# Hybrid decoder step: where in a unit's slot TensorE multiplies the next unit's attention scores

## The reference, cut to what matters

```python
n = rms_norm(x, g_mix)
q, k, v, xr, gr, gates = jnp.split(n @ w_in, SPLITS, axis=-1)
attn = attend(q, k, v, sb_bias)            # stick-breaking attention, 16 heads of 64, 4 kv heads
xc, rnn_buf_new = causal_dwconv(xr, rnn_buf, w_rnn_conv, b_rnn_conv)
hseq, h_last = rg_lru(xc, rnn_h0, w_rgate, b_rgate, w_igate, b_igate, rglru_lambda)
rnn = hseq * jax.nn.gelu(gr)
gate_a, gate_b = jnp.split(jax.nn.sigmoid(gates), 2, axis=-1)
x = x + (gate_a * attn + gate_b * rnn) @ w_out
# then a causal ConvFFN: up-projection, depthwise conv, gelu(ua) * ub, down-projection

def stick_breaking_weights(z, mask):       # z = q.k * scale + bias
    log_keep = jnp.where(mask, jax.nn.log_sigmoid(-z), 0.0)
    later = jnp.concatenate([log_keep[..., 1:], jnp.zeros_like(log_keep[..., :1])], axis=-1)
    tail = lax.cumsum(later, axis=z.ndim - 1, reverse=True)
    return jnp.where(mask, jnp.exp(jax.nn.log_sigmoid(z) + tail), 0.0)
```

## Time and profile before

| | |
|---|---|
| median of 3 runs | 2100.93 us |
| the profiled execution | 2100.63 us |
| its span, first to last instruction | 2098.9 us |
| TensorE busy / VectorE / ScalarE / GpSimd | 1902.7 / 1217.0 / 930.9 / 222.5 us |
| mean granted TensorE clock | 0.958 |

### The profile page before, as it was taken

How to read it: one execution, slowest core, us unless ns; L and a number is a source line. 1 busy time by engine, 2 the same in 40 slices (tenths; PEclk the granted TensorE clock), 3 DMA queues, 4 the chain that set the end, 5 groups by cost and what they waited for, 6 DMA issues and landing times. The chain is left out here.

```text
span 2098.9 us, 40932 instructions
## 1 busy us (share of the span) xinstructions
PE 1902.7 (91%) x14580; PEld 1739.5 (83%) x14580; DVE 1217.0 (58%) x1991; ACT 930.9 (44%) x1506; POOL 222.5 (11%) x106
## 2 busy tenths in 40 slices
PE   6998999899897989798995996999999999999985
PEld 5897878688786878687883776999999999999984
DVE  6101667567584858577677333655665566546645
ACT  5112676666767676667666211312222122221213
POOL 0121000000000000000003002311221122212210
PEclk9999999999998999999898997999999999999998
DMA  3334222131313232231312311211110111111104
GB/s 130 113 83 115 75 72 74 51 98 40 93 42 103 57 79 67 79 80 40 84 44 101 103 72 49 61 41 40 50 60 30 43 57 50 43 37 50 50 10 178
DMA packets 198716, 143.82 MB, mean 69 GB/s; under 512 B 58289, under 2 KB 187890, under 8 KB 198528
## 3 DMA queue, kind: packets, MB, share of 16 engines
q1 hardware_dynamic: 198554, 141.73, 23.0%
HBM read 124.31 MB, written 17.61 MB: 68 GB/s over the span
## 5 line engine op out<-in xcount | busy, mean ns | idle before, releaser
L87 PE MATMUL d_p_up<-n_hi,d_w_hi 128*128 128x346 f32 x1056 | 342.2, 324 | 15.9 <-ACT d_up L1808 8.3
L87 PE MATMUL d_p_up<-n_hi,d_w_lo 128*128 128x346 f32 x1056 | 341.6, 323 | 0.0
L87 PE MATMUL d_p_up<-n_lo,d_w_hi 128*128 128x346 f32 x1056 | 341.3, 323 | 0.0
L1911 DVE TENSOR_TENSOR mix<-mix,d_p_down 128x346 f32<-128x346 f32 x264 | 136.2, 516 | 267.7 <-PE d_p_down L1960 267.7
L87 PE MATMUL b_p_proj<-n_hi,b_w_hi 128*128 128x350 f32 x768 | 267.8, 349 | 6.8 <-ACT r_gr L1045 6.8
L87 PE MATMUL b_p_proj<-n_lo,b_w_hi 128*128 128x350 f32 x768 | 254.1, 331 | 0.0
L87 PE MATMUL b_p_proj<-n_hi,b_w_lo 128*128 128x350 f32 x768 | 253.4, 330 | 0.0
L1808 ACT ACTIVATE d_up<-d_p_up 128x346 f32<-128x346 f32 x132 | 60.2, 458 | 401.4 <-PE d_p_up L87 401.4
L87 PEld LDWEIGHTS d_p_up<-n_hi,d_w_hi 128*128 128x128 f32 x1056 | 200.7, 190 | 17.2 <-ACT d_up L1808 9.1
L87 PEld LDWEIGHTS d_p_up<-n_lo,d_w_hi 128*128 128x128 f32 x1056 | 201.1, 190 | 0.0
L87 PEld LDWEIGHTS d_p_up<-n_hi,d_w_lo 128*128 128x128 f32 x1056 | 200.8, 190 | 0.0
(11 more groups left out here) (262 smaller groups left out, 3872.1 us busy)
## 6 DMA issues: line engine op xcount, KB each, us to landing
w_raw<-in_w_in SPq DMA_DIRECT2D x45, 512.0 KB, 4.7
w_raw<-in_w_up SPq DMA_DIRECT2D x45, 512.0 KB, 3.8
b_page<-in_cache_k SPq DMA_DIRECT2D x128, 128.0 KB, 2.1
b_page<-in_cache_v SPq DMA_DIRECT2D x128, 128.0 KB, 2.1
w_raw<-in_w_down SPq DMA_DIRECT2D x22, 512.0 KB, 3.2
b_q_in<-q_scr SPq DMA_DIRECT2D x272, 32.0 KB, 2.2
mix<-in_x_prompt SPq DMA_DIRECT2D x8, 512.0 KB, 7.5
w_raw<-in_w_out SPq DMA_DIRECT2D x8, 512.0 KB, 3.2
```

Source lines behind the costliest of these rows:

```text
L87: last = pe.matmul(out, w[:, k, :], x[:, k, col:col + width], start=(k == 0 and w is w_hi and x is x_hi), stop=(k == KT - 1 and w is w_lo))
L1911: dve.tensor_tensor(to, to, p_down[:, n % 4, 0:FW], ALU.add).then_inc(down_out, 1)
```

## The change

`scores(s+1)` moves from the end of the slot to the place directly behind the projection burst, ahead of the gate product, the third group of transposed weights and the page work. Where the next unit is unit 16 (slot 9), it stays at the end, since a part of that unit's scores goes into the PSUM tile of the page transposes. Slot 16 has no next unit, and the first scores of a turn stay at its start. So 15 of 17 slots of a turn change.

```diff
                         for piece in PLACES[s]:
                             project_piece(i, *piece)
+                        if s + 1 < SLOTS and BLOCK_ORDER[s + 1] < 16:
+                            scores(i, s + 1)
                         if s in GATE_AT:
                             project_piece(i, GATE_AT[s], 0, KT)
                         for n in range(2, groups):
                             turn(i, v, n)
                         decode(i, s, first)
-                        if s + 1 < SLOTS:
+                        if s + 1 < SLOTS and BLOCK_ORDER[s + 1] == 16:
                             scores(i, s + 1)
```

## The result

The changed kernel takes 2121.32 us (median of 3 runs, 2119.09 to 2121.92) against 2100.93: a ratio of 1.0101, interval [1.0075, 1.0127], about 20 us. The forecast was 2105.5 with a range to 2113. The sign is right, the size is not.

The account below looks back on a forecast made before the run. TensorE, busy 1902.7 of 2098.9 us, was taken as the bound, so its waits decide. The terms -9.6 + 4.0 + 7.6 + 2.9 = +4.9 us on 2100.63 gave 2105.5 us, range 2096 to 2113.

Parts of the forecast that it names:

- Step 1: Slots 7 to 11: scores(8) start 1.37 earlier, shortening the waits in slots 10 and 11; 9.6 us gained over seven turns.
- Step 2: Slot 15 and the turn's boundary: value pages come second, delaying SyncE's requests by 0.57 at seven boundaries; 4.0 us lost.
- Step 3: Slots 0 and 1, and fresh turns' values: value pages follow the wait, key page requests and odd values late; 7.6 us lost.
- the clock rival: Behind slot 0, more idle time lowers the granted clock behind scores(1): 5.3 us more in seven turns, 2110.8 us; chance 0.18.
- the absorbed case: SyncE's queue absorbs the late requests: step 3 costs 1.2, step 4 nothing; sum -4.4, 2096.2 us; chance 0.20.
- Step 4: Page scores and gate products now behind the scores' narrow mask product, 96 places at 0.03 each; 2.9 us lost.

Follow-up runs that it names:

- slot 7 alone: Only the scores of slot 8 move (in slot 7, behind the burst), against the kernel before: 2091.3 us, ratio 0.9961 [0.9946, 0.9977].
- slot 15 alone: Only the scores of slot 16 move, ahead of slot 15's gate product and value pages, against the kernel before: 2101.27 us, ratio 1.0003.
- slot 0 alone: Only the scores of slot 1 move, so the last value pages follow them, against the kernel before: 2110.26 us, ratio 1.0056 [1.0034, 1.0078].
- the 64x64 pair: Kernel before plus two extra 64x64 products in each of 64 places: behind the burst 2121.87 us, ratio 1.0108; at the slot's end 2101.08 us, 0.9998.

## Why the prediction was wrong, step by step

- **Step 1 was right for slot 10, and not for slot 11.** -9.6 forecast; with slot 7 alone slot 10's wait is gone and the time falls by 8.2 us, its own junctions included. The chain from the scores over ScalarE to VectorE's weight copy is as told. But the r_gr wait was to fall to 0.5 by that chain and fell only to 0.85, 6.1 us in place of 6.8. In the changed kernel it is 3.5, and some of that is slot 10 being 0.19 longer, as above. So it is partly luck that the 9.9 us of its two lists lies so near to 9.6. Another detail was off: ScalarE's wait in slot 8 was to shrink to 0.5 on the scores. It is now 0.87 on VectorE, since the score copy also needs a free target.
- **Step 2 was wrong in size, as far as slot 15 alone shows.** +4.0 forecast; slot 15 alone shows +0.6 (-2.3 to +3.6), and in the changed kernel the wait for keys fell from 21.1 to 19.5. TensorE's side happened as told: in slot 15 of turn 3 the pages now start 1.32 behind the burst, before it was 0.68. The boundary did not get later by that. Which part of SyncE's chain takes it up was not tried. One thing stays open. In the five kernels that add work in slots 4 to 14 and leave slot 15 alone, the boundaries (from the burst of slot 16 to the next turn's values) are 3 to 10 us shorter over eight turns, one trace each; in the changed kernel they are 3.0 longer. Whether moving slot 15 takes that cover away, no run tests.
- **Step 3 was right in its causes, low in size.** +7.6 forecast, +11.8 (7.1 to 16.4) with slot 0 alone, so the forecast lies inside the interval. Turn 2 after the change, TensorE at slots 0, 1 and 4:

```profile
429.47 0.84 PE L1313 MATMUL b_p_z<-b_k_in,b_q_in 64*64 64x168 f32 x8 [4.77 <-ACT b_z L1026]
...
430.29 1.09 PE L1374 MATMUL b_p_kt<-b_page,b_zd 128*32 128x256 f32 x8
...
456.04 1.55 PE L1351 MATMUL b_p_misc<-b_w_t,b_v_odd 128*64 128x64 f32 x24 [3.42 <-DMA b_v_odd<-v_scr]
```

SyncE's queue, the key pages of that slot, and the clock behind scores(1) in turns 2, 3 and 6:

```profile
431.56 3.21 SPq L894 DMA_DIRECT2D b_page<-in_cache_k  x4
```

```profile
429.40:433.00 3.60, 3.53 (x37) 2.30 (x38) 0.29 (x2) 3.57 (x6) 0.00 (x0) 0.50 0.08 26
550.20:553.80 3.60, 3.60 (x41) 2.95 (x42) 1.10 (x4) 3.57 (x6) 0.00 (x0) 0.65 0.45 120
908.80:912.40 3.60, 3.53 (x41) 2.72 (x41) 0.87 (x3) 3.57 (x6) 0.00 (x0) 0.62 0.23 66
```

The wait for the odd values is 3.42, forecast 3.5. The request stands 431.56 - 429.47 = 2.09 behind scores(1); before it stood 425.67 - 422.86 = 2.81 ahead of them. That is 4.9 later, forecast 4.2. In turns 4 and 6 that wait is 2.88 and 2.11 (before 1.42 and 0.54); with slot 0 alone it is 0.72 in turn 6, so other moved slots may have a part in it. What I missed is that the pages, once behind the wait, can run at the lower clock. Here the granted clock is 0.50 (1.2 GHz) and they take 1.09, not 0.67. The prediction's sign for the clock rival did appear: behind scores(1) the granted clock fell in turns 1, 2, 3 and 5 (in turn 3 from 1.00 to 0.65) and rose in turns 6 and 7 (in turn 6 from 0.50 to 0.62). Its price did not. From scores(1) to the end of slot 1's burst the seven turns take 5.3 us longer in sum, and 7 x 0.67 = 4.7 of that are the value pages themselves, which leaves 0.6 for the clock. (The 1.2 of the absorbed case, step 3's lower bound, has no working.)
- **Step 4 failed, and with it the forecast.** I sized it 2.9 us: 0.03 in each of 96 places, "a small loss". The runs show 0.19 in 88 places without a wait, 17 us. Three things were wrong. I priced one junction, behind the scores (0.11 is what it is), and not the one ahead of them (0.09), where small tiles follow the projection. I argued the 0.11 down to 0.03, since the mask product has 64 columns and so lies "nearer to 350-column work". A 64-column product costs the page scores 0.06 even in their own shape, and the change of shape another 0.05. The earlier trace rows had the right number, for a reason that I did not see: its 2-column products are in 128\*64 tiles. (Those page scores of slot 3 had that price already and pay nothing more in turns 1 to 7; slot 1, at 0.15, and slot 12, at 0.20, pay and were left out.) And I let waits hide a third of the places: in slots 4 to 15 the changed kernel has one wait a turn left, the 0.5 for r_gr behind slot 10.

The sum with the sizes that showed, each from its own run or trace: -9.9 + 0 + 11.8 + 17 = +18.9, against the 20.4 measured. It fits better than its terms are known (11.8 alone is 7.1 to 16.4). The two profiled executions, from start to start of TensorE's products, give +18.5 at the junctions, -11.2 around the waits of slots 10 and 11, +11.7 in the rest of slots 0 to 4 and +3.0 at the boundaries: 22.0, against 2121.92 - 2100.63 = 21.3 between them.

The rule that I weighed in step 4 was not the one that decides. The Trainium skill, TensorEngine Tiling (Array Packing), Key Properties, says: "Mode switching requires drain: Changing tiling mode (not just tile) drains the TensorE". The trace agrees that a change has a price: what follows a change of shape starts 0.25 behind a 350-column product where the same shape starts 0.16 behind it, and the 64x64 pair costs 0.45 among 128x128 products and 0.07 among 64x64 ones. The page gives no price; here the moved scores pay about 0.13 us for one change more. The rule of the forecast, the Trainium skill, TensorE: Matmul & The Clock Gate, Part 3 (The mechanism), is that a weight load is pulled ahead of matmuls in flight when its row group does not conflict or it goes to the background buffer. I had left the condition out and read it as making the second junction free. The trace disagrees with that reading: the page scores behind the mask product take 0.92 to the transposes, and behind a short product of their own shape 0.87, not 0.81.

## What to carry to other kernels

When a block of small tiles is moved in TensorE's stream, write down the tile shape of its neighbours, before and after, and count the changes; look also at which work loses a long product in front. Here each place with one change more cost 0.19 us, and 88 of them without a wait cost more than the waits gained. Move only the instance whose consumer is late (here slot 7), not all that look alike. When total wait is unchanged and busy time grows with the same count of instructions, look at the junctions, not at the queues.

## What the runs showed that I had not expected

- One change more of the weight tile's shape went with 0.19 us, the clock at 1.00 and the work identical: 0.13 by the shape, 0.06 by a short product in front of the page scores. Two changes around extra products cost 0.22 to 0.38.
- Where the count of changes and the short neighbour were there already (slot 3 of turns 1 to 7), the moved scores cost 0.00.
- Products in 64\*64 tiles next to others of that shape are nearly free: two float32 products, four rows, added 0.07 to 0.12 a place, and 64 places could not be told from none.
- One 128x128 float32 product of 64 columns shows as two rows and costs 0.23 among products of its own shape, 0.06 of it in the work behind it.
